# Five raw weight buffers and three split pairs in place of three and four, in a two-model transformer kernel

## The chip, the cores and the metric

The kernel runs on one core of one Trainium2 chip. Its time is the device time of one execution in microseconds; three runs of the kernel before took 1712.07, 1713.02 and 1713.61 us (median 1713.02). TensorE (PE) multiplies matrices, VectorE (DVE), ScalarE (ACT) and GpSimd (POOL) work element by element, and SyncE (SP) gives out most of the loads.

## The reference

Two models of depth 2 run one after the other on 256 tokens with 1024 features in fp32. What is computed, cut to its steps (`h` is the residual stream, `norm` the RMS norm with a gain):

```
first:  h += hgrn2(norm(h));  h += swiglu(norm(h))
        h += attention(norm(h));  h += swiglu(norm(h));  h = norm(h)
second: h += 0.5 swiglu(norm(h));  h += short_conv(norm(h));  h += 0.5 swiglu(norm(h))
        k, v = compressed, selected and windowed keys and values from norm(h)
        h += 0.5 swiglu(norm(h));  h += sparse_attention(norm(h), k, v);  h += 0.5 swiglu(norm(h))
swiglu(x) = (silu(x @ Wg) * (x @ Wu)) @ Wd      with Wg, Wu 1024 x 2816, Wd 2816 x 1024
hgrn2: a gated linear recurrence over 8 heads, computed over levels of blocks (1, 2, 4, ... tokens)
```

The kernel keeps the accuracy of fp32 by splitting: each operand x is a high part (x rounded to the matmul's number type) and a low part (x minus the high part), and a product is high*high + high*low + low*high.

## The kernel before

The 256 tokens are two row tiles of 128 (t = 0, 1). All weights pass through in chunks of 128 x 2048 numbers (1 MB), one after the other in one fixed order, the same on every engine. The phases are hgrn, ffn0, moba (the first attention), ffn1, final, ffn2, conv, ffn3, kv, ffn4, nsa (the sparse attention), ffn5. A chunk goes this way:

- SyncE loads it into a raw buffer, `raw[n % RING]` (L511 to L522). Chunk n waits until chunk n - RING is split in both parts (semaphores `split_hi`, `split_lo`).
- ScalarE copies it into the high part, `whi` (L662). Split s waits for its load and until TensorE has used the chunk that was split WRING splits before (L661, semaphore `chunk_used`).
- VectorE subtracts the high part from the raw chunk into `wlo` (L1173).
- TensorE multiplies with both and adds one to `chunk_used` with the last matmul that reads the chunk. Four chunks, those of the compression in nsa (`w1`), are used raw, without a split.

Every engine runs its own list in order. There is no planner: where a split stands between other work is written out in the phase functions of each engine. These places matter:

- End of an FFN (ScalarE L729 on, VectorE L1230 on, TensorE L1862 on). The last chunks are u10, d9, d10 (up projection 10, down projection 9 and 10), then the next phase's first two, here called f0 and f1. TensorE does d9 and d10 for row tile 0, then both for row tile 1, and d9 is used up in the middle of tile 1. ScalarE's order is split d10, split f0, the high part of the last hidden tile, split f1, then the squares for the norm. VectorE's is split d10, split f0, the last hidden product (L1239), its low part (L1243), half of split f1, two additions into h (L1252), the other half, the normalisation (L1195). TensorE's transposes of the normalised tile (`turn`, L1815) stand before the last three matmuls of d10.
- End of a mixer (`out_product`). The output weights are four chunks, out0 to out3. TensorE goes through out2 and out3 once for each row tile, so both stay in use. ScalarE and VectorE split f0 and f1 before they turn to the additions and the norm.
- hgrn. Its eight levels for each half of the heads go back and forth: scores on TensorE (L1948), a level step on VectorE (L1335, L1337), which lets the next scores go. Halves of weight chunks (q, f, then og0 to og3) are multiplied between the scores, and splits stand between the level steps.
- The start. The masks (L536) are loaded behind hgrn's chunk number 6 (counted from 0).

Of the kernel before, what the change touches and what calls it, by code (L numbers as in the profile page):

```python
# [25 lines left out]
D = 1024  # L26
KT = D // P
CW = 256
RING = 3
WRING = 4  # L30
HEADS = 8
F_FF = 2816
PAIRS = F_FF // CW
# [82 lines left out]
class Chunks:  # L116
# [19 lines left out]
    def landed(self, n):  # L136

        return 16 * sum(self.transfers[n % RING:n + 1:RING])

# [76 lines left out]
def build(nc, w, out):  # L216

    with ExitStack() as ctx:
        def sb(name, shape, dt=F32):
            return ctx.enter_context(nc.sbuf_tensor(name, shape, dt))  # L220

        def sem(name):
            return ctx.enter_context(nc.semaphore(name))
# [3 lines left out]

        raw = [sb(f"raw{n}", [P, 2048]) for n in range(RING)]
        whi = [sb(f"whi{n}", [P, 2048], F32R) for n in range(WRING)]
        wlo = [sb(f"wlo{n}", [P, 2048], F32R) for n in range(WRING)]  # L230
        h = sb("h", [P, TT, D])
# [98 lines left out]

        landed = [sem(f"chunk_landed{n}") for n in range(RING)]
        split_hi = sem("split_hi")
# [170 lines left out]
        def _(sp):  # L503
            at = Place()

            def load(src, *key):
# [3 lines left out]
                at.chunk += 1  # L510
                if n - RING in chunks.direct:  # L511
                    sp.wait_ge(chunk_used, n - RING + 1)
                elif n >= RING:
                    sp.wait_ge(split_hi, chunks.split_number[n - RING] + 1)
# [135 lines left out]
        def _(act):  # L650
            at = Place()

            def split(*key, width=2048):
# [5 lines left out]
                act.wait_ge(landed[n % RING], chunks.landed(n))  # L659
                if s >= WRING:  # L660
                    act.wait_ge(chunk_used, chunks.of_split[s - WRING] + 1)  # L661
                act.activation(whi[s % WRING][:, 0:width], raw[n % RING][:, 0:width], ACT.Copy).then_inc(split_hi, 1)  # L662

# [487 lines left out]
        def _(dve):  # L1151
# [9 lines left out]
            def split(*key, width=2048, parts=(0, 1)):  # L1161
# [9 lines left out]
                else:  # L1171
                    part = slice(parts[0] * width // 2, (parts[0] + 1) * width // 2)
                ins = dve.tensor_tensor(wlo[s % WRING][:, part], raw[n % RING][:, part], whi[s % WRING][:, part].bitcast(F32), ALU.subtract)  # L1173
                if 1 in parts:
# [1134 lines left out]
```

## Time and profile before

| | |
|---|---|
| median of three runs | 1713.02 us |
| profiled execution, whole | 1713.76 us |
| its span on the core | 1712.0 us |
| TensorE busy (matmuls) | 1675.0 us, 98% |
| VectorE busy | 942.4 us, 55% |
| ScalarE busy | 721.1 us, 42% |
| `wlo` on VectorE, x270 | 601.4 us |
| `whi` on ScalarE, x265 | 497.8 us |
| HBM read | 290.75 MB, 171 GB/s over the span |

Busy is the time in which an engine runs an instruction; idle time of an engine that is not the bottleneck costs nothing. TensorE overlaps the loading of its left operand with the matmul before, and its matmuls with each other, so the distance from start to start tells more than the length of one. The granted clock is the share of full speed that TensorE was given; it has two levels here, 2.4 GHz (1.00) and 1.2 GHz (0.50).

### The profile page before, as it was taken

Reading aid. Unit: us, or ns where it says so; the run is one execution under the profiler, and the core shown is the slowest. Engines: PE = TensorE matmul, PEld = TensorE weight load, DVE = VectorE, ACT = ScalarE, POOL = GpSimd, SP = SyncE. Lnnn points to the kernel's source line nnn. Section 1 sums busy time; section 2 is a strip of 40 time slices with the busy share of each in tenths; the row PEclk is TensorE's granted clock in tenths of the full one; section 3 lists DMA queues with packets and bytes.
Section 4 is the critical chain, followed back from the end, with each engine's and each line's share of the span. In section 5 each row is a group of like instructions: output and inputs, shape, how many; then the busy total and the mean of one; then the engine's idle time right before and its main releaser. Section 6 shows DMA issues by size and latency. Waiting matters only on the chain.

```text
span 1712.0 us, 26152 instructions
## 1 busy us (share of the span) xinstructions
PE 1675.0 (98%) x11441; PEld 1528.4 (89%) x11445; DVE 942.4 (55%) x929; ACT 721.1 (42%) x822; POOL 60.0 (4%) x73
## 2 busy tenths in 40 slices
PE   8999999999999999999999999999999998899999
PEld 6898889989889998999989899998999986689998
DVE  4677644555565455554576545455545486754544
ACT  4433433444444344433353434345434334753432
POOL 0023000000000000000000000000000020000000
PEclk9899999999999999999999999999999999999999
DMA  6633557646364644655565554656564535046462
GB/s 215 197 124 99 192 147 228 213 164 197 127 205 155 215 161 167 214 194 175 183 207 168 173 204 159 210 173 200 193 217 153 188 117 167 1 136 209 154 215 74
DMA packets 221124, 295.05 MB, mean 172 GB/s; under 512 B 7517, under 2 KB 184881, under 8 KB 221011
## 3 DMA queue, kind: packets, MB, share of 16 engines
q1 hardware_dynamic: 215546, 284.40, 49.8%
q10 hardware_dynamic: 5464, 9.00, 2.1%
q8 instruction: 90, 1.47, 0.4%
q14 instruction: 24, 0.19, 0.0%
HBM read 290.75 MB, written 1.57 MB: 171 GB/s over the span
## 4 chain that ended last, share of the span: by engine, by line
PE 88%; DVE 6%; ACT 3%; issue 1%; DMA 1%; SPq 0%; POOL 0%; ACTq 0%; DVEq 0%; POOLq 0%
PE ps L1876 20%; PE ps L1773 16%; PE ps L1776 16%; PE ps L1774 16%; PE ps L1789 3%; PE ps L1799 3%; PE ps L1791 3%; DVE wlo L1173 3%; PE ps L1948 2%; ACT whi L662 2%; PE ps L1824 1%; PE ps L1825 1%; PE ps L1826 1%; PE ps L1815 1%; PE ps L2199 1%
## 5 line engine op out<-in xcount | busy, mean ns | idle before, releaser
L1173 DVE TENSOR_TENSOR wlo<-raw,whi 128x2048 fp32r<-128x2048 f32 (+2 forms) x270 | 601.4, 2247 | 221.0 <-ACT whi L662 219.7
L1773 PE MATMUL ps<-xhi,whi 128*128 128x256 f32 x2432 | 601.3, 285 | 7.1 <-DVE arena L1314 7.1
L1774 PE MATMUL ps<-xhi,wlo 128*128 128x256 f32 x2432 | 598.1, 283 | 0.0
L662 ACT ACTIVATE whi<-raw 128x2048 fp32r<-128x2048 f32 (+1 forms) x265 | 497.8, 1901 | 90.4 <-PE ps L1826 16.3
L1773 PEld LDWEIGHTS ps<-xhi,whi 128*128 128x128 f32 x2432 | 467.5, 192 | 10.5 <-DVE arena L1314 7.3
L1774 PEld LDWEIGHTS ps<-xhi,wlo 128*128 128x128 f32 x2432 | 467.9, 192 | 2.3
L1776 PE MATMUL ps<-xlo,whi 128*128 128x256 f32 x2432 | 342.1, 283 | 0.0
L1776 PEld LDWEIGHTS ps<-xlo,whi 128*128 128x128 f32 x2432 | 314.5, 192 | 0.0
L743 ACT ACTIVATE hhi<-hid 128x512 fp32r<-128x512 f32 x54 | 34.1, 632 | 491.2 <-DVE hid L1239 441.5
L1239 DVE TENSOR_TENSOR hid<-silu,ps 128x512 f32<-128x512 f32 x60 | 41.2, 687 | 299.8 <-PE ps L1776 299.8
L1876 PE MATMUL ps<-whi,hhi 128*128 128x512 f32 x480 | 187.6, 391 | 1.7 <-DVE hlo L1243 1.7
L1876 PE MATMUL ps<-wlo,hhi 128*128 128x512 f32 x480 | 187.5, 391 | 0.0
L1876 PE MATMUL ps<-whi,hlo 128*128 128x512 f32 x480 | 186.7, 389 | 0.0
L1876 PEld LDWEIGHTS ps<-whi,hhi 128*128 128x128 f32 x480 | 90.4, 188 | 19.1 <-DVE hlo L1243 1.9
L1876 PEld LDWEIGHTS ps<-whi,hlo 128*128 128x128 f32 x480 | 90.1, 188 | 19.2
L1876 PEld LDWEIGHTS ps<-wlo,hhi 128*128 128x128 f32 x480 | 90.4, 188 | 16.5
L1789 PE MATMUL ps<-whi,xhi 128*128 128x512 f32 x240 | 94.1, 397 | 3.4 <-ACT whi L662 1.2
L1791 PE MATMUL ps<-wlo,xhi 128*128 128x512 f32 x232 | 90.4, 390 | 0.0
L1243 DVE TENSOR_TENSOR hlo<-hid,hhi 128x512 fp32r<-128x512 f32 x54 | 37.4, 692 | 65.7 <-ACT hhi L743 65.7
L1799 PE MATMUL ps<-whi,xlo 128*128 128x512 f32 x240 | 62.0, 393 | 0.0
L737 ACT ACTIVATE silu<-ps 128x512 f32<-128x512 f32 x60 | 35.9, 598 | 56.3 <-PE ps L1776 56.3
L1789 PEld LDWEIGHTS ps<-whi,xhi 128*128 128x128 f32 x240 | 45.3, 190 | 15.6 <-issue 4.6
(232 smaller groups left out, 1294.9 us busy)
## 6 DMA issues: line engine op xcount, KB each, us to landing
raw<-in_ffn_w_gate_up SPq DMA_DIRECT2D x80, 1024.0 KB, 5.6
raw<-in_ffn_w SPq DMA_DIRECT2D x62, 1024.0 KB, 5.8
raw<-in_ffn_w_down SPq DMA_DIRECT2D x44, 1024.0 KB, 5.6
raw<-in_hgrn_w_in SPq DMA_DIRECT2D x16, 1024.0 KB, 5.5
raw<-in_moba_w_in SPq DMA_DIRECT2D x12, 1024.0 KB, 5.2
raw<-in_conv_w_in SPq DMA_DIRECT2D x10, 1024.0 KB, 5.6
raw<-in_ffn_w_gate_up SPq DMA_DIRECT2D x16, 512.0 KB, 4.9
raw<-in_kv_w SPq DMA_DIRECT2D x6, 1024.0 KB, 5.1
```

The source lines that it names most:

```text
L662: act.activation(whi[s % WRING][:, 0:width], raw[n % RING][:, 0:width], ACT.Copy).then_inc(split_hi, 1)
L737: act.activation(silu[:], by_two(ps[:, 4, :]), ACT.Silu).then_inc(silu_ready, 1)
L1173: ins = dve.tensor_tensor(wlo[s % WRING][:, part], raw[n % RING][:, part], whi[s % WRING][:, part].bitcast(F32), ALU.subtract)
L1239: dve.tensor_tensor(hid[:], silu[:], by_two(ps[:, 5, :]), ALU.mult).then_inc(hid_ready, 1)
L1243: dve.tensor_tensor(dst, src, high.bitcast(F32), ALU.subtract).then_inc(hlo_ready, 1)
L1773: pe.matmul(out, hi[:, k, tile], xhi[:, k, :], start=k == 0, stop=False)
L1774: pe.matmul(out, lo[:, k, tile], xhi[:, k, :], start=False, stop=False)
L1776: mm = pe.matmul(out, hi[:, k, tile], xlo[:, k, :], start=False, stop=k == KT - 1)
L1789: pe.matmul(out, xhi[:, k, tile], hi[:, k % 4, :], start=k == 0, stop=False)
L1791: pe.matmul(out, xhi[:, k, tile], lo[:, k % 4, :], start=False, stop=False)
L1799: mm = pe.matmul(out, xlo[:, k, tile], parts[k // 4][0][:, k % 4, :], start=False, stop=k == KT - 1)
L1876: mm = pe.matmul(out, a[:, k, tile], b[:, k, part], start=first and k == 0 and n == 0, stop=last and k == 1 and n == 2, skip_group_check=True)
```

## The change

RING, the number of raw buffers, goes from 3 to 5, and WRING, the number of pairs of high and low parts, from 4 to 3. A raw buffer is 2048 fp32 numbers a partition (8 KB), a pair two of that: 3 x 8 + 4 x 16 = 88 KB before, 5 x 8 + 3 x 16 = 88 KB after.

```diff
@@ -26,8 +26,8 @@
 D = 1024
 KT = D // P
 CW = 256
-RING = 3
-WRING = 4
+RING = 5
+WRING = 3
 HEADS = 8
 F_FF = 2816
 PAIRS = F_FF // CW
```

No instruction moves on any engine; the buffers that are named and the numbers that are waited for differ. On SyncE's queue, at the start of the program, the loads of hgrn's weights stood before like this (`rows` are small parameters, `const` the masks, brackets the semaphores of a load's wait):

```order
L522 DMA raw<-in_hgrn_w_in 128x8x256
L528 DMA rows<-in_hgrn_out_norm 8x128
L528 DMA rows<-in_hgrn_lb_logits 16x128
L530 DMA rows<-in_conv_w 24x128
L531 DMA rows<-in_cmp_b_2 4x128
L532 DMA rows<-in_cmp_pos 32x128
L522 DMA raw<-in_hgrn_w_in 128x8x256 [waits split_lo,split_hi] x3
L522 DMA raw<-in_hgrn_w_in 128x4x512 [waits split_lo,split_hi]
L536 DMA const<-in_masks 128x1340
```

And now, at the same place of the same queue:

```order
L522 DMA raw<-in_hgrn_w_in 128x8x256
L528 DMA rows<-in_hgrn_out_norm 8x128
L528 DMA rows<-in_hgrn_lb_logits 16x128
L530 DMA rows<-in_conv_w 24x128
L531 DMA rows<-in_cmp_b_2 4x128
L532 DMA rows<-in_cmp_pos 32x128
L522 DMA raw<-in_hgrn_w_in 128x8x256 x2
L522 DMA raw<-in_hgrn_w_in 128x8x256 [waits split_lo,split_hi]
L522 DMA raw<-in_hgrn_w_in 128x4x512 [waits split_lo,split_hi]
L536 DMA const<-in_masks 128x1340
```

Two loads, chunks 3 and 4, have lost their wait, and the two behind them wait for earlier splits than before (of chunks 0 and 1, not 2 and 3); the masks follow them directly. On ScalarE's queue the row of a split reads the same in both kernels, for its wait has the same semaphore and another number.

## Rows read from the trace of the kernel before

**Rows 1.** The page, parts 1 and 4: busy time, and the chain that ended last

```profile
PE 1675.0 (98%) x11441; PEld 1528.4 (89%) x11445; DVE 942.4 (55%) x929; ACT 721.1 (42%) x822; POOL 60.0 (4%) x73
...
PE 88%; DVE 6%; ACT 3%; issue 1%; DMA 1%; SPq 0%; POOL 0%; ACTq 0%; DVEq 0%; POOLq 0%
```

**Rows 2.** The page, part 5: operation, count, busy us, mean ns, idle before it

```profile
L1173 DVE TENSOR_TENSOR wlo<-raw,whi 128x2048 fp32r<-128x2048 f32 (+2 forms) x270 | 601.4, 2247 | 221.0 <-ACT whi L662 219.7
...
L662 ACT ACTIVATE whi<-raw 128x2048 fp32r<-128x2048 f32 (+1 forms) x265 | 497.8, 1901 | 90.4 <-PE ps L1826 16.3
```

**Rows 3.** Timeline of ACT, end of ffn0: start us, us, operation, idle before

```profile
356.11 3.70 ACT L662 ACTIVATE whi<-raw 128x2048 fp32r<-128x2048 f32 x2
...
363.70 1.90 ACT L662 ACTIVATE whi<-raw 128x2048 fp32r<-128x2048 f32 x1
```

**Rows 4.** Timeline of DVE, end of ffn0

```profile
358.04 4.49 DVE L1173 TENSOR_TENSOR wlo<-raw,whi 128x2048 fp32r<-128x2048 f32 x2 [2.63 <-ACT whi L662]
362.45 0.68 DVE L1239 TENSOR_TENSOR hid<-silu,ps 128x512 f32<-128x512 f32 x1
363.83 0.69 DVE L1243 TENSOR_TENSOR xlo<-hid,xhi 128x512 fp32r<-128x512 f32 x1 [0.70 <-ACT xhi L743]
365.63 1.22 DVE L1173 TENSOR_TENSOR wlo<-raw,whi 128x1024 fp32r<-128x1024 f32 x1 [1.11 <-ACT whi L662]
...
367.65 0.69 DVE L1252 SCALAR_TENSOR_TENSOR h<-ps,h 128x512 f32<-128x512 f32 x1 [0.19 <-PE ps L1876]
...
370.41 1.41 DVE L1195 SCALAR_TENSOR_TENSOR xn<-h,rstd,gain 128x512 f32<-128x512 f32 x2 [0.93 <-POOL rstd L1108]
```

**Rows 5.** Timeline of PE, end of ffn0

```profile
364.58 0.50 PE L1876 MATMUL ps<-whi,xhi 128*128 128x512 f32 x1 [0.50 <-DVE xlo L1243]
...
367.45 0.39 PE L1876 MATMUL ps<-whi,hhi 128*128 128x512 f32 x1
...
370.17 0.39 PE L1876 MATMUL ps<-whi,xhi 128*128 128x512 f32 x1
...
372.22 1.03 PE L1815 MATMUL ps<-const,xn 128*128 128x128 f32 x8
```

**Rows 6.** Timeline of DVE and PE, end of moba

```profile
473.91 4.49 DVE L1173 TENSOR_TENSOR wlo<-raw,whi 128x2048 fp32r<-128x2048 f32 x2 [1.11 <-ACT whi L662]
...
479.79 0.39 PE L1824 MATMUL ps<-whi,xhi 128*128 128x512 f32 x1
...
482.42 1.32 PE L1815 MATMUL ps<-const,xn 128*128 128x128 f32 x8 [0.42 <-DVE xn L1195]
```

**Rows 7.** Timeline of DVE and PE, hgrn, second half of the heads

```profile
140.14 1.13 DVE L1335 TENSOR_TENSOR arena<-arena 128x64 f32<-128x64 f32 x1
...
141.92 2.05 PE L1948 MATMUL ps<-arena 128*128 128x128 f32 x16 [0.94 <-DVE arena L1337]
```

**Rows 8.** Timeline of DVE and PE, nsa's query projection

```profile
1390.17 1.22 DVE L1584 TENSOR_REDUCE kss<-arena 128x16 f32<-128x1024 f32 x1
...
1394.51 0.47 PE L1789 MATMUL ps<-whi,xhi 128*128 128x512 f32 x1 [0.25 <-DVE wlo L1173]
```

**Rows 9.** Timeline of SP, DVE and PE, start of the program

```profile
28.47 1.40 SPq L536 DMA_DIRECT2D const<-in_masks  x1
...
37.55 0.23 DVE L1373 CAST ident_b<-const 128x128 bf16<-128x128 f32 x1 [3.87 <-DMA const<-in_masks]
...
46.30 0.58 PE L1773 MATMUL ps<-xhi,whi 128*128 128x256 f32 x1 [7.11 <-DVE arena L1314]
```

**Rows 10.** Timeline of PE, and windows (us, busy PE PEld DVE ACT POOL, clock, DMA, GB/s)

```profile
462.24 1.54 PE L2040 MATMUL ps<-const,arena 128*128 128x128 f32 x6 [2.43 <-DVE arena L1462]
...
462.00:465.00 3.00, 2.76 (x10) 2.47 (x11) 0.79 (x2) 1.18 (x2) 0.00 (x0) 0.50 0.90 250
...
48.00:52.00 4.00, 4.00 (x20) 4.00 (x20) 3.03 (x5) 1.91 (x1) 0.00 (x0) 0.50 1.06 353
52.00:56.00 4.00, 4.00 (x33) 4.00 (x33) 1.56 (x2) 0.97 (x2) 0.00 (x0) 0.95 0.96 282
```

## The prediction

> **What bounds the kernel now.** I read the busy shares and the chain of waits first: TensorE is busy 1675.0 of 1712.0 us, and its instructions are 88% of the chain that ended last [rows 1]. So a change helps only by what is left of TensorE's idle time, 37 us in all, and hurts by every microsecond it makes TensorE wait. Next the costliest groups: each weight chunk is split by a copy on ScalarE (`whi`, 1.90 us) and a subtraction on VectorE (`wlo`, 2.25 us on the mean, 2.29 at full width) [rows 2]. One after the other they take 4.2 us, with hand-overs 4.4 us, beside some 5.5 us of TensorE work for a chunk (24 matmuls of 0.227 us; the second and third of [rows 5] are 12 matmuls and 2.72 us apart). The idle time before `wlo` is nearly all behind ScalarE, and none of either row names a transfer as its main releaser: loads don't bound. Then I read the timeline where one phase goes over to the next, engine by engine [rows 3 to 5].
>
> **What the two numbers do.** Memory is equal (8 KB a partition for a raw chunk, 16 KB for a pair: 88 KB before and after), and no instruction is added or moved. Two waits change their number. SyncE loads chunk n when chunk n-5 is split, not n-3: earlier. ScalarE splits s when TensorE has used up s-3, not s-4: one chunk, 5.5 us, later. As ScalarE and VectorE run in order, what stands behind a waiting split waits too, and that is where I look.
>
> **Inside the FFN rounds: nothing.** In a round the split of the next g waits for the g that the silu behind it needs anyway; likewise u and the high part. From the use of s-3 TensorE has two chunks, 11 us, to do, and the split needs 4.4. Cost 0. What hides it are those two chunks; with one chunk of cover left it would still be hidden by 1 us.
>
> **The end of an FFN, first wait.** The chunks there are u10, d9, d10 and the first two of the next phase, f0 and f1. Before, ScalarE splits d10 and f0 in one go at 356.11 and VectorE their low parts from 358.04 to 362.53 [rows 3, 4]. Now f0 waits until u10 is used. TensorE starts d9 right behind u10, and 12 matmuls of it (2.72) stand before its wait of 0.50 at 364.58 [rows 5]: u10 is over at 364.58 - 0.50 - 2.72 = 361.36. ScalarE then needs 1.93 and VectorE 2.29 with the hand-overs, to 365.6. Only behind that comes the product of the last hidden tile, with its high and low parts: from 362.45 to TensorE's start at 364.58 they took 2.13. So 365.6 + 2.1 = 367.7. Cost 3.15 us.
>
> **The end of an FFN, second wait.** f1 now waits until d9 is used, in the middle of the second row tile: call that D (370.17 in [rows 5]). ScalarE is done at D+2.1, VectorE's first half (1.22) at D+3.3, the two additions that stand behind it (0.69 each) at D+4.6; from the end of the second addition to the normalisation passed 2.07 us (368.34 to 370.41, squares and root) [rows 4], and half of its 1.41 with the hand-over is 0.8: D+7.5. TensorE wants the transposes of it at D+2.05 (372.22) and had no wait. It idles 5.5 us, and 0.3 more as the second half comes late. Together 8.95 us at each of the five FFNs that something follows: 44.8 us. (ffn1, which normalises twice and has twelve filling matmuls, comes to 8.8 by the same sum.)
>
> **The end of a mixer.** The fourth chunk pair is held open there: out2 and out3 are both read twice. f1 waited for out1, now for out2, used at 479.79 plus 0.2. With 4.2 for the split it ends at 484.2, where VectorE had finished at 478.40; the transposes began 4.0 us behind that (482.42) after an idle 0.42 [rows 6]. So they begin at 488.2: 5.8 us here. In the three others TensorE did not wait, and the time is 6.5. Four mixers: 25.3 us.
>
> **hgrn's inner part.** VectorE has the splits of out0, out1, out2 in front of level steps that TensorE's scores wait for. Each now waits for the og chunk that TensorE finishes just before those scores. At 141.92 TensorE had waited 0.94, so og was over at 140.98; from the start of the level step to the scores are 1.78 us [rows 7]. Now 4.4 + 1.8 = 6.2 us of idle, 5.3 more than before; the third such place had no idle before its scores, and costs 5.6 with a shorter step (estimate); the first is partly covered, 1.5. In the first four heads the splits f2, og0, og1 come late by the same rule behind a little slack: I take 3 (estimate, between nothing and one chain of 4.4). Sum 15 us, bounds 8 and 18.
>
> **Four single places.** In nsa, q0 and q1 wait for the two chunks of the first projection, and between their low parts stand squares and sums on VectorE (1.22 the one in [rows 8], two such): q0's low part comes some 3.8 us late, 0.5 of which the slack before q1 takes up: TensorE, which already waited 0.25 at 1394.51 for q1, waits 3.3 more. In moba v1 must wait for f0, whose last use stands 12 matmuls (2.72) before v1 is wanted: 4.4 - 2.7 = 1.7. kv (f1 behind win0, with two evictions between) and conv (out2 ahead of the last product) I take at 2.1 each. Sum 9.3.
>
> **What is won.** At the start SyncE gives out the masks behind the seventh chunk, at 28.47, once chunk 3 is split; they are there at 37.55, and VectorE, 3.87 us idle for them, sets TensorE's 7.11 us of idle before 46.30 [rows 9]. With five buffers the seventh chunk needs only chunk 1 split, the masks go out two splits and a TensorE chunk earlier (about 10 us, estimate) and are there when VectorE comes: -3.9 us. The other early loads win nothing.
>
> **The clock.** After 2.43 us of idle the granted clock was 0.50 in 462 to 465, and work restarted at 462.24: 3 us at 1.2 GHz, 1.5 us lost. After 7.11 us of idle it was still 0.50 in 48 to 52, and 0.95 in the next 4 us: 6 us after the restart at 46.30, 3.0 us lost [rows 10]. New idles of 2.4 us or more: ten at FFN ends, four at mixer ends, two in hgrn, nsa, kv: 18. Between 1.5 and 3.0 I take the middle, 2.2, as the idles (3.9 to 6.4 us) lie between the two: 40 us, bounds 27 and 54, and 0 if the clock stays.
> The Trainium skill (TensorE: Matmul & The Clock Gate, What's actually happening) puts the penalty of the slow clock under 1% of a typical kernel's span. By it the clock would cost at most 17 us and the sum stand at 1821 or less; the trace of before agrees for itself, but it has few such idles, and the two priced here, times 18, give more.
>
> **Sum.** 44.8 + 25.3 + 15 + 9.3 - 3.9 = 90.5 us of waits, + 40 of clock = 130.5. The profiled execution took 1713.76 us (span 1712.0); the median of the runs is 0.74 less. 1713.0 + 130.5 = 1843.5, forecast 1844.
>
> **Rivals.**
> The cover holds: the splits end before they are wanted at the borders as well, as 4.4 us fits under two chunks. Then only the earlier masks count: 1713 - 4 = 1709, or 1706 if the clock recovers sooner: faster. It decides where TensorE has over 4.4 us between the signal and the taker. For it: all FFN rounds have 11 us. Against: at D it has 2.05 us, and the adds and squares queue behind. 4%.
> No change: with three pairs one free chunk of 5.5 us always lies between a use and the next need, more than 4.4, and the start gains nothing, as the levels behind it wait for other things: 1713, 2%. Against: out2 and out3 are held open together, which leaves a single pair free. The Trainium skill (Trainium Kernel Development and Optimization, Best Practices) asks for double buffering to overlap transfers with compute; by that rule three pairs are as good as four.
> The waits come, the clock stays: 1713 + 90.5 = 1804. For it: idles of under a microsecond [rows 7] leave no trace in the clock. Against: 2.43 us did. 8%.
> The waits come, but the hgrn part is hidden and the clock costs the lower 1.5 a stall: 1713 + 90.5 - 7 + 27 = 1824. 16%.
> A stall costs 3.0 of clock, slow matmuls delay the next signal in hgrn's chain too (+3): 1713 + 93.5 + 54 = 1860. 14%.
> The forecast, within 1828 to 1855: 56%.
>
> **Range and chances.** 0.2% (3.4 us) is about what a measurement here can tell from no change. Slower holds all but the first two rivals: 94%; same 3%; faster 3%. Range 1798 to 1866: it takes in the no-clock case and the dearest.
>
> **What would show it.** In the profile after: TensorE busy share near 93%; `whi` idle behind TensorE lines L1776, L1876 and L1826 instead of the old few; at each FFN end an idle of about 3.9 before the first matmul on `xhi` and about 5.5 before the transposes L1815; 6.4 before them at mixer ends; two idles of about 6 before L1948 in hgrn; the masks issued about 10 us earlier, the 7.11 before L1773 down to 3.3; clock digits under 9 where those idles lie. The rounds inside the FFNs unchanged. I would be wrong if the FFN rounds lengthened, if the border idles were below 2 us, or if loads showed up as a new wait.

## The result and the profile after

The changed kernel takes 1836.45 us (median of 4 runs, 1833.49 to 1837.61), the kernel before 1712.63 us beside it (4 runs, 1712.07 to 1713.61): a ratio of 1.0722, 95% interval 1.0709 to 1.0735, so slower by 124 us. The forecast was 1844 us, with a range of 1798 to 1866. The profiled execution took 1833.49 us, with a span of 1831.7 us at a mean granted clock of 0.966 (before: 1712.0 us and 0.992). Two single runs beside the experiments, one of the kernel before (6311.34 us) and one of the masks early (5855.25 us), took over three times as long; they count in the medians below and are left out of the ratios.

The page of the changed kernel, parts 1, 4 and 5, answers to [rows 1, 2]:

```profile
PE 1711.5 (93%) x11445; PEld 1555.0 (85%) x11445; DVE 942.6 (51%) x929; ACT 726.0 (40%) x822; POOL 61.0 (3%) x73
...
PE 86%; DVE 6%; ACT 5%; issue 2%; POOL 0%; DMA 0%; SPq 0%; ACTq 0%; DVEq 0%; POOLq 0%
...
L1173 DVE TENSOR_TENSOR wlo<-raw,whi 128x2048 fp32r<-128x2048 f32 (+2 forms) x270 | 606.7, 2248 | 621.8 <-ACT whi L662 620.8
L662 ACT ACTIVATE whi<-raw 128x2048 fp32r<-128x2048 f32 (+1 forms) x265 | 504.3, 1905 | 604.9 <-PE ps L1776 293.8
```

The splits themselves cost what they cost before (1905 and 2248 ns), and VectorE and ScalarE are busy as long. What grew is the idle time in front of them: ScalarE's from 90.4 to 604.9 us, now behind TensorE. That is cheap in itself, since ScalarE is no bottleneck. The price shows on TensorE: its idle time went from 37.0 us (1712.0 - 1675.0) to 120.2, which is 83.2 more, and its busy time rose by 36.5 us. No work was added, so those 36.5 are the same matmuls at the lower clock. The clock rows bear it out: summed over half microseconds, busy time times the missing share of the clock is 11.3 us before and 47.3 us after, 36.0 more. The two together are the 119.7 us between the spans.

The idle time by what TensorE waited for, from the view of waits of the changed kernel (total us, times, longest):

```profile
PE ps L1815 <- DVE xn L1195: 51.9, 9, 6.4
PE ps L1876 <- DVE xlo L1243: 18.2, 5, 3.6
PE ps L1948 <- DVE arena L1337: 14.3, 4, 5.1
PE ps L1789 <- DVE wlo L1173: 5.3, 3, 2.7
PE ps L2040 <- DVE arena L1462: 4.4, 7, 2.5
PE ps L1824 <- DVE xlo L1576: 4.4, 1, 4.4
PE ps L1773 <- DVE arena L1314: 3.3, 1, 3.3
PE ps L1789 <- ACT arena L1009: 2.2, 1, 2.2
```

The first two rows are the borders of the phases: nine waits before the transposes and five before the product of the last hidden tile (d10). Before, these were under 1 us each [rows 5, 6]. L2040 was there before. No row of TensorE's waits names a transfer.

The timelines of ScalarE, VectorE and TensorE at the end of ffn0, against [rows 3 to 5]:

```profile
384.79 1.92 ACT L662 ACTIVATE whi<-raw 128x2048 fp32r<-128x2048 f32 x1 [3.42 <-PE ps L1776]
...
398.54 1.92 ACT L662 ACTIVATE whi<-raw 128x2048 fp32r<-128x2048 f32 x1 [8.25 <-PE ps L1876]
```

```profile
386.73 2.29 DVE L1173 TENSOR_TENSOR wlo<-raw,whi 128x2048 fp32r<-128x2048 f32 x1 [3.05 <-ACT whi L662]
388.94 0.68 DVE L1239 TENSOR_TENSOR hid<-silu,ps 128x512 f32<-128x512 f32 x1
...
400.49 1.22 DVE L1173 TENSOR_TENSOR wlo<-raw,whi 128x1024 fp32r<-128x1024 f32 x1 [9.48 <-ACT whi L662]
401.63 1.28 DVE L1252 SCALAR_TENSOR_TENSOR h<-ps,h 128x512 f32<-128x512 f32 x2
...
404.96 1.41 DVE L1195 SCALAR_TENSOR_TENSOR xn<-h,rstd,gain 128x512 f32<-128x512 f32 x2 [0.92 <-POOL rstd L1108]
```

```profile
391.06 0.50 PE L1876 MATMUL ps<-whi,xhi 128*128 128x512 f32 x1 [3.63 <-DVE xlo L1243]
...
405.77 1.97 PE L1815 MATMUL ps<-const,xn 128*128 128x128 f32 x8 [5.29 <-DVE xn L1195]
```

Read it as a relay. At 384.79 ScalarE is let go by TensorE's last matmul on u10 and splits f0. VectorE takes the low part, and only at 388.94 multiplies the last hidden tile, whose inputs had been there since u10 was used up. TensorE, which needs that tile, stands from 387.4 to 391.06. The same again: d9 is used up, f1 is split at 398.54, half of its low part is ahead of the two additions at 401.63, and the normalisation comes at 404.96, for which TensorE stands 5.29 us.

The end of moba, answering to [rows 6]:

```profile
517.67 2.29 DVE L1173 TENSOR_TENSOR wlo<-raw,whi 128x2048 fp32r<-128x2048 f32 x1 [5.80 <-ACT whi L662]
...
523.96 1.97 PE L1815 MATMUL ps<-const,xn 128*128 128x128 f32 x8 [6.30 <-DVE xn L1195]
```

hgrn and nsa, timelines of TensorE, to [rows 7, 8]:

```profile
134.96 2.87 PE L1948 MATMUL ps<-arena 128*128 128x128 f32 x16 [3.12 <-DVE arena L1337]
...
146.57 3.50 PE L1948 MATMUL ps<-arena 128*128 128x128 f32 x16 [5.12 <-DVE arena L1337]
...
162.68 3.79 PE L1948 MATMUL ps<-arena 128*128 128x128 f32 x16 [5.07 <-DVE arena L1337]
...
1504.27 0.47 PE L1789 MATMUL ps<-whi,xhi 128*128 128x512 f32 x1 [2.70 <-DVE wlo L1173]
```

The start, timelines of SyncE's queue and of VectorE, to [rows 9]:

```profile
18.64 1.38 SPq L536 DMA_DIRECT2D const<-in_masks  x1
...
33.06 0.23 DVE L1373 CAST ident_b<-const 128x128 bf16<-128x128 f32 x1
```

The masks go out 9.8 us earlier (28.47 before), and VectorE no longer waits for them. The clock, to [rows 10], in windows after the two idles at the end of ffn0 (columns as there):

```profile
392.00:395.00 3.00, 3.00 (x9) 2.34 (x8) 0.00 (x0) 0.00 (x0) 0.00 (x0) 0.50 0.53 182
395.00:398.00 3.00, 3.00 (x13) 2.44 (x13) 0.00 (x0) 0.00 (x0) 0.00 (x0) 0.93 0.00 0
405.80:408.00 2.20, 2.20 (x10) 2.10 (x11) 1.18 (x2) 0.82 (x2) 0.00 (x0) 0.50 1.04 356
```

### The profile page after: what moved, and what is told of

It reads as the page before. It is cut to its first block, busy times and chain, and to the rows that moved or that the text cites. A ratio compares the mean times of both kernels' runs of the same rounds, so it can differ in the third digit from the quotient of the medians.

```text
span 1831.7 us, 26155 instructions
## 1 busy us (share of the span) xinstructions
PE 1711.5 (93%) x11445; PEld 1555.0 (85%) x11445; DVE 942.6 (51%) x929; ACT 726.0 (40%) x822; POOL 61.0 (3%) x73
## 3 DMA queue, kind: packets, MB, share of 16 engines
q1 hardware_dynamic: 215546, 284.40, 47.3%
## 4 chain that ended last, share of the span: by engine, by line
PE 86%; DVE 6%; ACT 5%; issue 2%; POOL 0%; DMA 0%; SPq 0%; ACTq 0%; DVEq 0%; POOLq 0%
PE ps L1876 19%; PE ps L1773 16%; PE ps L1774 16%; PE ps L1776 16%; PE ps L1789 3%; PE ps L1791 3%; PE ps L1799 3%; ACT whi L662 3%; DVE wlo L1173 3%; PE ps L1815 2%; PE ps L1824 1%; PE ps L1948 1%; PE ps L1826 1%; PE ps L1825 1%; PE ps L2199 1%
## 5 line engine op out<-in xcount | busy, mean ns | idle before, releaser
L1173 DVE TENSOR_TENSOR wlo<-raw,whi 128x2048 fp32r<-128x2048 f32 (+2 forms) x270 | 606.7, 2248 | 621.8 <-ACT whi L662 620.8
L662 ACT ACTIVATE whi<-raw 128x2048 fp32r<-128x2048 f32 (+1 forms) x265 | 504.3, 1905 | 604.9 <-PE ps L1776 293.8
L1876 PE MATMUL ps<-whi,hhi 128*128 128x512 f32 x480 | 188.8, 393 | 1.7 <-DVE hlo L1243 1.7
L1876 PE MATMUL ps<-wlo,hhi 128*128 128x512 f32 x480 | 188.3, 392 | 0.0
L1876 PE MATMUL ps<-whi,hlo 128*128 128x512 f32 x480 | 187.3, 390 | 0.0
L1876 PEld LDWEIGHTS ps<-whi,hhi 128*128 128x128 f32 x480 | 91.3, 190 | 19.7 <-DVE hlo L1243 1.9
L1876 PEld LDWEIGHTS ps<-whi,hlo 128*128 128x128 f32 x480 | 90.7, 189 | 19.5
L1876 PEld LDWEIGHTS ps<-wlo,hhi 128*128 128x128 f32 x480 | 91.1, 190 | 16.8
L1815 PE MATMUL ps<-const,xn 128*128 128x128 f32 x176 | 32.0, 341 | 51.9 <-DVE xn L1195 51.9
L1815 PEld LDWEIGHTS ps<-const,xn 128*128 128x128 f32 x176 | 26.8, 178 | 57.8 <-DVE xn L1195 55.7
```

The lines of the kernel that those rows point to most:

```text
L1815: mm = pe.transpose(ps[:, 4 + 2 * t + half, k * P:(k + 1) * P], xn[:, t, kk * P:(kk + 1) * P], ident)
L1876: mm = pe.matmul(out, a[:, k, tile], b[:, k, part], start=first and k == 0 and n == 0, stop=last and k == 1 and n == 2, skip_group_check=True)
```

## The experiments

The first four (three pairs, filling, first wait, all ends) stood beside runs of the kernel before with a median of 1712.41 us, the last four beside runs with one of 1712.84 us. In the cuts of code `...` stands for lines left out; where both engines change, one is shown.

### Three raw buffers, three pairs

```diff
-RING = 5
+RING = 3
 WRING = 3
```

> Three raw buffers as before, three pairs. Theory (late splits: the fourth pair carries the loss, the two more raw buffers only the earlier masks): as slow as the changed kernel plus the start, 1836.5 + 4.5 = 1841 us, with the masks issued at about 28 us again and the idle before 46.3 back at about 7 us. Rival (the deeper load ring costs time, by loads that crowd each other): near 1713 to 1725, with the idles at the FFN ends gone.

Measured: 1839.77 us (1838.54 to 1840.57), ratio 1.0746 (1.0729 to 1.0763). The pairs alone do the whole damage. Every wait of 2 us or more is that of the changed kernel, but for one:

```profile
PE ps L1773 <- DVE arena L1314: 7.9, 1, 7.9
```

It was 3.3 us with five buffers. The masks went out at 31.41 here and VectorE waited 4.70 us for them. So the two further raw buffers are worth the earlier masks, 3.3 us of time, and nothing else that the waits show.

### Filling the idles to hold the clock

The changed kernel, with matmuls on a tile of zeros that is there already, placed where TensorE waits at the borders (16 at the first wait, 23 before the transposes at FFN ends, in ffn1 beside its 12, and 27 at the ends of moba, conv and nsa). Their number is chosen to take less time than the wait.

```diff
+                    elif after:
+                        keep_warm(16)
                 pe.wait_ge(hlo_ready, hids + PAIRS)
...
-                        between = lambda: turn(after, 0)
+                        between = lambda: (keep_warm(23), turn(after, 0))
...
+                                if name != "hgrn":
+                                    keep_warm(27)
                                 turn(after, 0)
...
-                    keep_warm(WARM_FINAL)
+                    keep_warm(WARM_FINAL + 23)
```

> The changed kernel with filling matmuls on zeros (no part of the result) where TensorE waits at phase ends: 16 before the last hidden tile's product at five FFN ends, 23 before the transposes there (ffn1: beside its 12), 27 before the transposes at the ends of moba, conv and nsa; at 0.227 us each about as long as the idles of 3.63, 5.29 and 6.3 us. Theory (the slow clock after an idle is a cost by itself, beside the wait): the idles' clock periods there, some 75 of 124 us at the half level, vanish, about 29 us: 1808 us. Rival (only the wait costs, slow matmuls are hidden or harmless): no change, 1836.

Measured: 1813.13 us (1812.72 to 1814.53), ratio 1.0593 (1.0576 to 1.061), mean clock 0.986 instead of 0.966. Added work made the kernel 23 us faster, less than the 28 expected, and the rival (no change) is out. TensorE gets its data no sooner; it only does something in the meantime. A window behind the first wait at the end of ffn0:

```profile
391.00:394.00 3.00, 3.00 (x15) 2.45 (x14) 0.00 (x0) 0.00 (x0) 0.00 (x0) 1.00 0.61 212
```

15 matmuls in 3 us, against 9 in the changed kernel's window from 392 on. So the price of the clock is shown apart from the waits, and it is of the size of the extra busy time: 23 of 36.5 us. The same sum over the clock rows as above gives 22.3 us at the lower clock, 25.0 less than in the changed kernel. What is left lies where nothing was filled: hgrn and its end, conv, nsa and the start.

### The first wait undone

The split of f0 is put behind the last hidden tile on both engines, so that it holds up nobody. VectorE's part:

```diff
-                if after:
-                    split(after, "first", 0)
                 dve.wait_ge(hlo_ready, base + PAIRS - 1)
                 multiply(PAIRS - 1)
                 low_part(PAIRS - 1, xlo[:, 0:2, :], xhi[:, 0:2, :])
+                if after:
+                    split(after, "first", 0)
```

> The changed kernel, but at the FFN ends the split of f0 stands behind the last hidden tile's high part on ScalarE and behind its product and low part on VectorE, so nothing queues behind f0. Theory (a late split costs by what queues behind it): the idle of 3.63 falls to about 0 at five places and the five clock periods go with it: 5 x 3.6 + 11 = 29 less, but f1 is not moved: 1808 to 1812 us. Rival (TensorE lacks split pairs, whatever the order of the queues): f0 then comes later still and TensorE waits for it instead, 1836 or more.

Measured: 1807.4 us (1804.89 to 1808.98), ratio 1.0556 (1.054 to 1.0573). The row L1876 <- L1243 with its 18.2 us is gone; the others stand:

```profile
PE ps L1815 <- DVE xn L1195: 51.9, 9, 6.4
PE ps L1948 <- DVE arena L1337: 14.3, 4, 5.1
PE ps L1789 <- DVE wlo L1173: 5.3, 3, 2.7
```

So the cost was the place in the queue, not the lateness of f0, and the rival is out. 29 us came back for 18.2 us of idle. Nearly all of the rest is clock: TensorE's busy time fell from 1711.5 to 1701.8.

### All ends undone

With that, the split of f1 goes behind the additions and the normalisation of row tile 0 on VectorE, and behind its squares on ScalarE, at FFN ends (but ffn1) and mixer ends. The mixer ends on ScalarE:

```diff
-                for n in range(2):
-                    split(after, "first", n)
+                split(after, "first", 0)
                 for half in range(2):
                     squares(after, 0, half)
+                split(after, "first", 1)
                 squares(after, 1, 0)
                 x_high(after, 0)
```

> As first_wait_undone, and the split of f1 stands behind what it held up: on ScalarE behind the squares of row tile 0, on VectorE behind the additions and the normalisation of row tile 0; at the ends of ffn0, 2, 3, 4 and of all four mixers (ffn1 keeps the old order for f1). Theory (queueing): idles of 5.29 (four) and 6.3 (four) before the transposes go, with their clock, 46 + 20 us, less about 1 us at each of the eight places where the later f1 holds up the second row tile: 1751 us, range 1742 to 1762. Rival (lack of pairs): the waits come back before the along matmuls on f1, 1800 or more.

Measured: 1764.89 us (1760.21 to 1765.91), ratio 1.0302 (1.0282 to 1.0322). 43 us less than the run above, and 3 above the range expected. What was missed:

```profile
PE ps L1795 <- issue: 10.7, 4, 2.7
PE ps L1821 <- DVE xn L1197: 7.1, 5, 5.4
```

The 5.4 is ffn1, whose order was kept. At the four mixer ends the transposes come in time, but TensorE waits 2.7 us a little later, before its first matmul of the next phase. The end of moba, timelines of VectorE, ScalarE and TensorE:

```profile
502.74 2.29 DVE L1175 TENSOR_TENSOR wlo<-raw,whi 128x2048 fp32r<-128x2048 f32 x1 [0.64 <-ACT whi L662]
504.95 1.28 DVE L1213 TENSOR_TENSOR h<-ps,h 128x512 f32<-128x512 f32 x2
...
505.67 0.63 ACT L686 ACTIVATE xn<-h 128x512 f32<-128x512 f32 x1 [2.96 <-DVE h L1213]
506.29 1.06 ACT L692 ACTIVATE xhi<-ps 128x512 fp32r<-128x512 f32 x2
...
506.97 0.77 PE L1795 MATMUL ps<-whi,xhi 128*128 128x512 f32 x1 [2.66 <-issue]
```

That matmul needs f0, which is long split, and the high part of the normalised tile (`xhi`), and the view names no releaser for it. In the order of the code and in time it is again a queue: the split of f1 (its wait is for out2) is now in front of the additions of row tile 1 on VectorE; behind the first of these stands a square on ScalarE (L686), and behind the square the high part of row tile 0 (L692), which TensorE takes 0.7 us after it starts. At the other three mixer ends it is the same 0.7 us. The expectation had allowed 1 us for this at eight places; it was 2.7 at four and nothing at the FFN ends, where ScalarE takes the high part of row tile 0 ahead of the squares of tile 1. An order with the high part first was not run for mixers.

### hgrn's order

Three splits stand one or two level steps later on VectorE (and on ScalarE the high part of y stands ahead of the split of out0, which is not shown):

```diff
-                split(name, "out", 0)
                 low_y(0)
                 next_level(1, 3)
-                gate_o(1)
-                split(name, "out", 1)
+                split(name, "out", 0)
                 next_level(1, 4)
+                gate_o(1)
                 next_level(1, 5)
-                split(name, "out", 2)
+                split(name, "out", 1)
                 next_level(1, 6)
+                split(name, "out", 2)
                 next_level(1, 7)
```

> The changed kernel (RING 5, WRING 3) with one edit: in the second half of hgrn's heads VectorE does the splits of out0, out1 and out2 one or two level steps later (behind levels 3, 5 and 6), and ScalarE the high part of y ahead of the split of out0. Theory: the three idles of 3.12, 5.12 and 5.07 us before the scores L1948 are level steps that stand behind a split that waits for an og chunk; they go to under 1 us each: 13.3 us of idle and two to three slow stretches of clock of 1.5 to 2.2 us, so 1836.4 - 13.3 - 4 = 1819 us (1816 to 1824). Rival: the splits, done later, are wanted at once by the output product: then 4 us and more of idle appear before L1824 or L1795 there, and the time is 1828 to 1833.

Measured: 1815.26 us (1814.31 to 1817.79), ratio 1.0598 (1.0583 to 1.0612), just under the range expected. All three idles are gone, and two small ones are new:

```profile
148.61 0.47 PE L1824 MATMUL ps<-whi,hhi 128*128 128x512 f32 x1 [0.81 <-issue]
...
152.48 0.50 PE L1824 MATMUL ps<-whi,xhi 128*128 128x512 f32 x1 [0.87 <-DVE xlo L1365]
```

The output product wanted its splits hardly sooner than they came, so the rival is out: 3.12 + 5.12 + 5.07 - 0.81 - 0.87 = 11.6 us of idle, and 5.4 of busy time (1711.5 to 1706.1).

### All orders together

> The changed kernel (RING 5, WRING 3) with all three reorderings: that of the first wait and of f1's split at the ends of FFNs and mixers (1764.9 us measured) and that of hgrn's second half. Theory: the parts are independent, so this is 1764.9 less what the hgrn reordering alone gives (17): 1748 us, 36 above the kernel before; left are the 5.4 of ffn1, the single places of conv, nsa, kv and moba, the 2.7 at mixer ends, and their clock. Rival: the output product of hgrn, with f0 and f1 later as well, becomes late: 1755 or more.

Measured: 1742.3 us (1738.56 to 1743.43), ratio 1.0162 (1.0147 to 1.0178). 22.6 us less than without hgrn's order, so the parts add up, a little better than expected. Of the change's 124 us, the order of work on ScalarE and VectorE gives back 94. In the 29 that remain are 10.7 of idle at mixer ends and 5.4 at ffn1, which by the timelines are places in a queue too, the single places, and their clock. How much of the 29 another order could give back, and how much is the price of the missing pair, no run shows.

### The masks early, in the kernel before

Three raw buffers, four pairs, and one call moved on SyncE:

```diff
                     if i == 0:
                         parameters()
+                        masks()
...
-                    if n == 0:
-                        masks()
```

> The kernel before (RING 3, WRING 4) with one edit: SyncE gives out the masks right behind the small parameters, ahead of hgrn's chunk 3, and not behind chunk 6. Theory: all that five raw buffers gave is that the masks came earlier. Then this edit alone, with three raw buffers and four pairs, brings TensorE's idle of 7.11 us before L1773 down to about 3.3, and the time to 1712.4 - 3.9 = 1708.5 us, 1707 if the clock recovers sooner; the same step that separates the changed kernel from the run with three raw buffers and three pairs (3.3 us). Rival: the masks (0.7 MB) compete with the first weight chunks and delay them by as much as they gain: 1712, with new idle time before L1789 in the first 20 us.

Measured: 1709.96 us (median of 11 runs), against 1712.84 (21 runs); ratio 0.9977 (0.9968 to 0.9986). This is the best version, 0.2% faster than the kernel before. VectorE's wait is gone and TensorE's is the changed kernel's 3.29. The 3.8 us of idle gave 2.9 us of time, and some 30 us earlier another wait is longer:

```profile
12.86 1.68 PE L1788 MATMUL ps<-whi,xhi 128*128 128x512 f32 x4 [2.08 <-ACT xhi L691]
...
43.58 0.39 PE L1772 MATMUL ps<-xhi,whi 128*128 128x256 f32 x1 [3.29 <-DVE arena L1313]
```

The first wait was 0.82 before. That the masks' transfer does this is not shown: the same wait is 1.77 in the changed kernel, which gives the masks out only at 18.64, and 0.6 to 2.0 in the runs made from it, which start as it does. So the expectation's rival (the masks delay the first weights by as much as they gain) is out as a whole, and open as a small share.

### The masks early and the FFN order

The same, with the order of "The first wait undone" in the kernel with four pairs.

> The kernel before (RING 3, WRING 4) with the masks early as in the other run and, at the end of the FFNs, the split of f0 behind the last hidden tile's high part on ScalarE and behind its product and low part on VectorE. Theory: the wait of 0.50 us before the first matmul on the last hidden tile, five times, goes as well, since the hidden tile no longer stands behind a split that nobody wants yet: 1708.5 - 2.5 = 1706 us. Rival: f0's low part, 2.1 us later, makes the additions and the normalisation late: the same 2.5 us come back before the transposes L1815, 1708.5 or more.

Measured: 1710.87 us (1708.78 to 1713.37), ratio 0.9986 (0.9978 to 0.9995), no better than the masks alone. The rival was right, as the waits say (L2039 and L1814 are the changed kernel's L2040 and L1815):

```profile
PE ps L2039 <- DVE arena L1461: 4.5, 7, 2.4
PE ps L1814 <- DVE xn L1194: 4.1, 7, 0.7
```

The 2.5 us before the last hidden tile went, and before the transposes there are 4.1 us, where the masks alone had 0.6; 0.7 is the longest. An order that is worth 29 us with three pairs is worth nothing with four.

## Why the prediction was right, point by point

| step | predicted us | in the trace us |
|---|---|---|
| FFN rounds | 0 | 0: the one idle of 0.8 us or more in them, 1.72 in ffn0, is in both kernels (its clock is not the same, see the last section) |
| FFN ends, first wait, x5 | 15.8 | 15.7: 5 x (3.63 - 0.50) |
| FFN ends, second wait, x5 | 29.0 | 26.6: 4 x 5.29 + 5.40 |
| mixer ends | 25.3 | 24.9: 6.40 + 6.30 + 6.29 + 6.31 - 0.42 |
| hgrn | 15 | 11.8: 14.3 - 2.5 |
| single places | 9.3 | 9.6: nsa 3.3, moba 1.8, kv 2.2, conv 2.3 |
| start | -3.9 | -3.8: 3.29 - 7.11 |
| sum of the waits | 90.5 | 84.8 by these rows, 83.2 in all |
| clock | 40 | 36.5 |
| together | 130.5 | 119.7 in the profiled runs, 124 in the medians |

- **The first wait** was right to 0.02 us a place (the list of signs says an idle of 3.9, the sum itself 3.15 + 0.50). The two chains (1.93 + 2.29 of f0's split, then 2.13) could be read off the timeline of before, and first_wait_undone confirmed that the queue is the cause.
- **The second wait** was 0.5 us too dear at four places and 0.3 at ffn1. The sum let the second half of the normalisation cost 0.3 of its own, and the chain from D to the transposes is a little shorter than 7.5. A term mis-sized, not a wrong mechanism.
- **The mixer ends**: 5.8 and 6.5 were predicted, 5.9 and 6.3 to 6.4 measured. The 5.8 has its rows; the 6.5 of the three others was given no working. What the prediction did not see is a second queue behind the split of f1, by way of the additions of row tile 1. That showed only when the first was taken away.
- **hgrn**: the idles were to be about 6.2 and 5.6, and were 5.12 and 5.07; the first, called partly covered at 1.5, was 1.5 more (3.12 for 1.59). The 3 us for the first four heads were 1.0 (one idle of 1.01 at 77.42). The 1.5, the 5.6 and the 3 were estimates without rows. The 6.2 had them, and two terms were too long: the level step L1335 took 1.13 us in [rows 7] and 0.22 at the same place after (145.69), so that from its start to the scores passed 0.88 and not 1.78; and from the end of the og chunk (141.45) to that step 4.24 and not 4.4. 4.24 + 0.88 is the 5.12 measured. Why the step was longer before stays open. hgrn was the term most off.
- **The start** was right in mechanism and size; w3_only and masks_early show it twice. In time it gave 3.3 and 2.9 us.
- **The clock**: 2.2 us for each of 18 idles gave 40 against 36.5, and warm_fill shows that this part is real. The count was near by luck. There are nineteen new idles of 2.4 us or more, 1.9 us of busy time each on the mean: hgrn has three and not two, conv's 2.08 grew to 4.37 and was not counted, and kv, which was, idled 2.23 and kept the full clock. The Trainium skill (TensorE: Matmul & The Clock Gate, What's actually happening) says of the ramp to the full clock that it costs under 1% of a typical kernel's span. The kernel before agrees (11.3 of 1712.0 us, 0.7%). The changed kernel does not: the added part alone is 36.5 of 1831.7 us, 2.0%, for it starts anew nineteen times more, and the 1821 or less that the prediction worked out by that page was too low.
- **The rivals**: "the cover holds" and "no change" fell with the first profile. With out2 and out3 both held open, and d9 until the middle of row tile 1, three pairs are not as good as four. "The clock stays" (1804) fell by warm_fill. The forecast came out 8 us high, in the profiled runs 10.8 (130.5 against 119.7): hgrn was 3.2 too dear, the clock 3.5, the second wait 2.4, and 1.6 us of waits went away that no row of the table has. That the errors are small against 124 us is the merit of the sum; that the clock's is among them is luck.

## What to carry to other kernels

Here a ring that is one buffer shorter cost no waits in the steady rounds and a great deal at the borders. Look there for the instruction that waits for the buffer, and list what is queued behind it and who waits for that. If the work behind it does not need the buffer, move it ahead: that gave back 94 of 124 us here. Then look again, for a second queue can stand behind the first, as at the mixer ends. When a change gives one ring more and takes from another, run each alone; the gain of the first may be had with one moved line.

## What was not expected of the hardware

**The same idle does not always cost the same.** In the changed kernel the idle of 3.63 us at the end of ffn0 was followed by a clock of 0.50 from 392 to 395. In the run with hgrn's order, the same place with the same idle kept the full clock. Its timeline of TensorE:

```profile
372.05 0.50 PE L1876 MATMUL ps<-whi,xhi 128*128 128x512 f32 x1 [3.63 <-DVE xlo L1243]
```

Its windows behind that:

```profile
372.00:375.00 3.00, 2.95 (x13) 2.45 (x14) 0.00 (x0) 0.00 (x0) 0.00 (x0) 1.00 0.86 299
375.00:378.00 3.00, 3.00 (x15) 2.49 (x14) 0.00 (x0) 0.12 (x1) 0.00 (x0) 1.00 0.00 0
```

It goes the other way too. The idle of 1.72 us in ffn0 is the same in both kernels; the kernel before keeps the full clock behind it, the changed kernel does not. The windows from 0.9 us behind the restart, before and after:

```profile
254.30:257.30 3.00, 3.00 (x15) 2.46 (x14) 2.84 (x2) 2.42 (x3) 0.00 (x0) 1.00 0.72 150
276.00:279.00 3.00, 3.00 (x9) 2.32 (x8) 2.81 (x2) 2.43 (x3) 0.00 (x0) 0.50 0.80 166
```

And the idle of 2.43 us in moba that priced the lower bound, followed by 0.50 in [rows 10], is 2.45 us in the changed kernel, with the full clock behind it:

```profile
499.00:502.00 3.00, 2.56 (x15) 2.24 (x16) 0.98 (x3) 1.65 (x2) 0.00 (x0) 1.00 0.81 271
```

So a price for each idle is a mean over many, and a single place can't be foretold from its length. What decides stays open: no run here varied the moment alone. The term of 40 us was near because it was taken over eighteen of them and its miscounts cancelled.
